# Two transformer-like blocks on one core: the order of the attention heads' vector work, the wait ahead of the first head, and one product for the position bias

## The chip, the cores and the metric

The kernel runs on one core of a Trainium2 chip. The metric is the device time of one execution in microseconds (us). The kernel before takes 866.2 us (median of 3 runs, 864.95 to 867.63).

## The reference, cut to what matters

The program computes a block of three parallel branches (local attention with a position bias, retention, attention to a memory), a gated feed-forward part with a short convolution, and after it two more layers. Sequence length is 256, model width 1024. The change lies in the first block's first stage. What is computed there, shortened:

```
n = rmsnorm(x, g_mix)
q_a, k_a, v_a, q_r, k_r, v_r, g_r, q_m, z_a, z_r, z_m = split(n @ w_in)
# local attention, 8 heads of 64; one block of 256 covers the whole sequence
s_own = q_a @ k_a.T * 64**-0.5 + table[:, rel_bucket(i - j)]   # table = rel_bias.T, 32 buckets x 8 heads
s_own = where(i >= j, s_own, -1e30);  y_a = softmax(s_own) @ v_a
# retention, 4 heads of 128: scores * decay, @ v, then a normalization of each row (mean, variance)
# memory attention, 4 heads of 128: softmax(q_m @ k_m.T * 128**-0.5) @ v_m
merged = sigmoid(z_a) * (y_a @ w_br_attn) + sigmoid(z_r) * (y_r @ w_br_ret) + sigmoid(z_m) * (y_m @ w_br_mem)
```

The position bias of a head is a function of i - j alone: a row of 384 numbers holds it for all distances that occur, and the 128 x 256 tile that a head adds is that row, read with a start that moves by one from partition to partition.

## The kernel before, in words

All large products run on TensorE in single-precision parts: each weight piece (128 x 2048 numbers, 1 MB) is loaded into `raw`, ScalarE (ACT) writes its rounded high part `whi` (L1117), and VectorE (DVE) subtracts to get the low part `wlo` (L1603). TensorE makes three passes over each piece (L452 to L454 where tokens lie on the output's partitions): 24 matmuls of 512 columns. There are 124 pieces, in a ring of three buffers. The cast of piece p+2 waits until piece p-1 has been multiplied; the subtraction waits for the cast; the load of the piece that reuses the buffer, issued from SyncE (SP), waits for the subtraction (L431).

Every engine runs one loop over the same steps, one step for each piece, in an order written out by hand. Step p is what stands ahead of and beside piece p. Pieces 0 to 3 are the memory's keys and values, 4 to 19 the first eight 512-wide chunks of `w_in` (two pieces each; chunk 0 is q_a, 1 is k_a, 2 is v_a), 20 to 31 its gates, 32 to 37 the branches' output products.

The heads run in a pipeline beside the pieces. There are 16 of them: local heads 0 to 7 start at steps 10 to 17, retention heads at 18 to 21, memory heads at 22 to 25. A head that starts at step n is turned (transposed) at step n, scored at n+1, its probabilities are turned at n+2 (not for retention), and it is weighed with the values at n+3. TensorE does, at the start of step p and ahead of piece p: `head_weigh` (L706), `head_prob_turn` (L684), `head_score` (L658 to L665), `head_turn` (L639), and each waits for what it needs from the step before. Vector work of step p is `head_dve(p)` (L1823): it normalizes the head that was weighed (for retention heads a chain of some twenty small operations, L1831 to L1844), adds the bias and takes the maximum of the head that was scored (L1866 to L1875; L1860 and L1872 for the other kinds), and copies the turned head out of PSUM (L1880). ACT's `head_act` takes the exponentials (L1271) and copies the turned probabilities (L1263). In DVE's loop the subtraction stands ahead of the head work:

```
                if p not in LATE_SPLIT:
                    split(p + 2)
                head_dve(p)
```

`head_turn` of the first head waits for ACT to have emptied chunk 2 of `w_in` (L625), the values, which piece 9 ends.

The position bias is made in steps 3 to 9, a head in each of steps 3 to 8 and two in step 9 (`rel_heads`). For each head GpSimd (POOL) copies its column of the table to 128 columns (`relw`, L2238), TensorE multiplies that with a constant 33 x 384 selection (`rel_rows`, L718), so that all 128 rows of the result are equal, ACT copies it to `brows` (L1254) and POOL stores it to memory as 128 rows (L2241). Two heads share the buffers by turns; TensorE's next product waits for ACT's copy of the last (L715), ACT's copy waits for the store before the last (L1253). After all eight, POOL loads each head's 128 x 256 tile `bias` from memory with rows that start one number apart (L2251). The first use of `bias` is DVE's at step 11 (L1865).

Of the kernel before, what the change touches and what calls it, by code (L numbers as in the profile page):

```python
# [15 lines left out]
P = 128  # L16
D = 1024
S = 256
T = S // P
# [59 lines left out]
def c0(name):  # L79
    return FIRST[name][1]  # L80
# [58 lines left out]
    return None  # L139


def rel_heads(n):


    return {9: (6, 7)}.get(n, (n - 3,) if 3 <= n < 9 else ())


LATE_SPLIT = (p0("up"), p0("xp") - 1, p0("xp"), p0("xp") + 1, p0("cu") - 1, p0("cu"), p0("cu") + 1)
# [13 lines left out]
def program(nc, ins, out):  # L162
    ctx = ExitStack()
    with ctx:
        def sb(name, shape, dt=F32):
            return ctx.enter_context(nc.sbuf_tensor(name, shape, dt))
# [4 lines left out]
        def overlay(size, *groups):  # L171

            made = []
            for group in groups:
# [44 lines left out]
        [[bias, decay, rcos, rsin, onehot, brows], [poolb, mtri, mmla, invf, sel, rows, csin, ccos, ang, kpr]] = overlay(  # L219
            8192 + RET_H * TRI * 4 + 1024 + 3 * TRI * 4,  # L220
            [("bias", [P, MOBA_H, S], F32), ("decay", [P, RET_H, TRI], F32), ("rcos", [P, T, 64], F32),
             ("rsin", [P, T, 64], F32), ("onehot", [P, TRI], F32), ("brows", [P, 2, TRI], F32)],
            [("poolb", [P, 4, T, S], F32), ("mtri", [P, S], F32), ("mmla", [P, TRI], F32),
             ("invf", [P, 32], F32), ("sel", [P, ML_H, P], F32),
             ("rows", [8, 5, S], F32),
# [3 lines left out]
        par = sb("par", [P, NPAR])  # L229
        half = sb("half", [P, 20])  # L230
        relb = sb("relb", [P, MOBA_H])
        relw = sb("relw", [P, 2, P])
        stats = sb("stats", [P, 32])
        rstd = sb("rstd", [P, 32])
        hrstd = sb("hrstd", [P, 3, T])
# [16 lines left out]
        qss = sb("qss", [P, T, MLA_H])  # L252
        kpss = sb("kpss", [P, T])
        rqk = sb("rqk", [P, 2, T, MLA_H])

        ones = relw[:, 0, :]

        hm = [qk_t[:, i, :].rearrange("p (t d) -> p t d", t=T) for i in range(2)]

# [26 lines left out]
        s_memt = [s_memt, sem("mem_columns_loaded_2")]  # L286
        s_ss, s_turn, s_thi, s_tlo = (sem(n) for n in (
            "squares_summed", "turned", "turned_hi", "turned_lo"))
        s_rb, s_rbw, s_rbs, s_bias = (sem(n) for n in (
            "rel_rows", "rel_lhs", "rel_rows_copied", "bias_loaded"))  # L290
        s_rbd = [sem(f"rel_rows_stored{i}") for i in range(2)]
        s_jt, s_jte, s_js, s_jse, s_jx, s_jp, s_jpe, s_jo, s_jn = (sem(n) for n in (
            "head_turned", "head_turned_copied", "head_scored", "scores_biased", "probs_ready",
            "probs_turned", "probs_turned_copied", "head_weighed", "head_done"))
# [27 lines left out]
        s_memset = sem("memset")  # L322
        s_store = sem("out_stored")

        scratch = nc.dram_tensor("bias_rows", (MOBA_H, P * TRI), F32, kind="Internal").ap()

        def pcol(name, i=0):
# [119 lines left out]
        def _(pe):  # L447
# [167 lines left out]
            def head_turn(p):  # L615

                if head_at(p) is None:
                    return
                kind, h = head_at(p)
                j = job(kind, h)  # L620
                if j not in TURNED:
                    return
                n = TURNED.index(j)
                if kind == "moba" and h == 0:
                    chunk_free(pe, c0("qkv") + 2)  # L625
                if kind == "ret" and h == 0:
                    pe.wait_ge(s_rot, 1)
                if kind == "mem" and h == 0:
                    chunk_free(pe, c0("qkv") + 7)
                if n >= 1:  # L630
                    pe.wait_ge(s_jte, n)
                else:
                    pe.wait_ge(s_rbs, MOBA_H)
                    pe.wait_ge(s_ident, 16)
                qs, ks = {"moba": (0, 1), "ret": (3, 4), "mem": (7, 8)}[kind]
                c = slice((h // 2 if kind == "moba" else h) * P, (h // 2 if kind == "moba" else h) * P + P)
                for i, s_ in enumerate((qs, ks)):
                    for t in range(T):
                        ins_ = nc.tensor.transpose(A[0][:, i * S + t * P:i * S + t * P + P],  # L639
                                                   tok[:, s_, t, c], ident[:, :])  # L640
                ins_.then_inc(s_jt, 1)
# [46 lines left out]
            def head_weigh(p):  # L688
                if head_at(p - 3) is None:
                    return  # L690
                kind, h = head_at(p - 3)
                j = job(kind, h)
                if j >= 1:
                    pe.wait_ge(s_jn, j)
                if kind == "ret":
                    pe.wait_ge(s_jse, j + 1)
                    chunk_free(pe, c0("qkv") + 5)
                    src = [(0, 0, 0), (1, 0, P), (1, 1, 2 * P)]
                    buf, vs, w = prob[:, j % 2, :], 5, P
                else:  # L700
                    pe.wait_ge(s_jpe, SMAX.index(j) + 1)
                    src = [(t, k, i * P) for i, (t, k, _) in enumerate(prob_blocks(kind))]
                    buf = prob_t[:, SMAX.index(j) % 2, :]
                    vs, w = (2, 64) if kind == "moba" else (9, P)
                for i, (t, k, col) in enumerate(src):
                    last = mm(A[3][:, t * P:t * P + w], buf[:, col:col + P],  # L706
                              tok[:, vs, k, h * w:h * w + w],
                              start=k == 0, stop=i + 1 == len(src) or src[i + 1][0] != t)
                last.then_inc(s_jo, 1)

            def rel_rows(h):

                pe.wait_ge(s_rbw, h + 1)
                if h >= 1:
                    pe.wait_ge(s_rbs, h)  # L715
                else:
                    pe.wait_ge(s_c1, 32)
                mm(A[3][:, 0:TRI], relw[0:33, h % 2, :], onehot[0:33, :],  # L718
                   start=True, stop=True).then_inc(s_rb, 1)


            def gate_logits():
                pe.wait_ge(s_gl, 1)
# [238 lines left out]

            first_piece()
            for p in range(1, Z0):
                for h in rel_heads(p):
                    rel_rows(h)
                head_weigh(p)
                head_prob_turn(p)
                head_score(p)
# [131 lines left out]
        def _(act):  # L1101
# [145 lines left out]
                                                        ACT.Copy, scale=gain(name, 2 * i + j))  # L1247
                    last.then_inc(s_thi, 1)

            def rel_copy(h):  # L1250
                act.wait_ge(s_rb, h + 1)
                if h >= 2:
                    act.wait_ge(s_rbd[h % 2], 16 * (h // 2))  # L1253
                nc.scalar.copy(brows[:, h % 2, :], A[3][:, 0:TRI]).then_inc(s_rbs, 1)  # L1254

            def head_act(p):

# [272 lines left out]
            for p in range(Z0):  # L1530
                if p not in LATE_SPLIT:
                    split(p + 2)
                empty(p - 1, True)
                for h in rel_heads(p):
                    rel_copy(h)
                head_act(p)
                ml_act(p)
                xc_act(p)
# [49 lines left out]
        def _(dve):  # L1588
# [588 lines left out]
            for p in range(Z0):  # L2177
                if p == p0("uq"):
                    mla_k()
                late(p)  # L2180
                if p == ML0 + 6:
                    ya_lo(p)
                if p not in LATE_SPLIT:
                    split(p + 2)
                head_dve(p)
                ml_dve(p)
                if p < ML0 + 6:
                    ya_lo(p)
                xc_dve(p)
                gates_dve(p)  # L2190
                if p == 2:
                    input_lo("mix", range(4))
                if p == 20:
                    dve.wait_ge(s_gh, 1)
                    V.tensor_tensor(wglo[:, :, :], wgate[:, :, :], wghi[:, :, :].bitcast(F32),
                                    ALU.subtract).then_inc(s_gl, 1)
                if p == p0("aout") - 1:
                    angles()
                boundary(p)
                for name, step in SCALED.items():  # L2200
                    if step == p:
                        normed(name)
                for name, which in turn_steps(p):
                    turn_lo(name, which)
                if p0("pool") - 3 <= p <= p0("pool"):
                    b = p - (p0("pool") - 3)
                    dve.wait_ge(s_mixhi, b + 1)
                    V.tensor_tensor(x1lo[:, 2 * b:2 * b + 2, :].rearrange("p k s -> p (k s)"),
                                    A[2 + b % 2][:, :],
                                    x1hi[:, 2 * b:2 * b + 2, :].rearrange("p k s -> p (k s)").bitcast(F32),  # L2210
                                    ALU.subtract).then_inc(s_mixlo, 1)
                if p == p0("ukv"):
                    mla_pe_k()
                if p == p0("uq") + 2:
                    mla_q_pe()
                empty(p)
# [4 lines left out]
        def _(pool):  # L2221
# [6 lines left out]
                i.then_inc(s_pool, 1)  # L2228
                pool.wait_ge(s_pool, count[0])

            Q.memset(relw[32:33, :, :], 1.0).then_inc(s_memset, 1)
            pool.wait_ge(s_memset, 1)

            pool.wait_ge(s_rel, 16)
            for h in range(MOBA_H):
                if h >= 2:
                    pool.wait_ge(s_rb, h - 1)
                Q.tensor_copy(relw[0:32, h % 2, :], relb[0:32, h:h + 1].broadcast_to([32, P])).then_inc(s_rbw, 1)  # L2238
                if h >= 1:
                    pool.wait_ge(s_rbs, h)  # L2240
                    pool.dma_start(scratch[h - 1].rearrange("(p n) -> p n", p=P), brows[:, (h - 1) % 2, :])\  # L2241
                        .then_inc(s_rbd[(h - 1) % 2], 16)
            pool.wait_ge(s_rbs, MOBA_H)
            Q.memset(ones, 1.0).then_inc(s_memset, 1)
            pool.dma_start(scratch[MOBA_H - 1].rearrange("(p n) -> p n", p=P), brows[:, (MOBA_H - 1) % 2, :])\
                .then_inc(s_rbd[(MOBA_H - 1) % 2], 16)
            for i in range(2):
                pool.wait_ge(s_rbd[i], 16 * MOBA_H // 2)

            for h in range(MOBA_H):  # L2250
                pool.dma_start(bias[:, h, :], scratch[h, P - 1:P - 1 + P * (TRI - 1)]  # L2251
# [210 lines left out]
```

## Time and profile before

| what | value |
|---|---|
| median of 3 runs | 866.2 us |
| the profiled execution's own time | 867.28 us |
| its span, first to last instruction | 865.5 us |
| mean granted TensorE clock | 0.982 of full |
| TensorE matmuls busy | 813.2 us (94%) |
| DVE, ACT, POOL busy | 566.2, 434.6, 141.5 us |

The span is some 1.8 us shorter than the execution's own time; this is what lies around the instructions. A TensorE busy for 94% of the span with a clock at 98% says that what can be won without less arithmetic lies in its gaps, in matmuls that could be left out, and in stretches at the lower clock. Times in the timeline count from the span's start.

### The profile page before, as it was taken

To read this page: it belongs to the slowest core of one execution; us is meant where nothing else is said; L and a number is where in the kernel's file an instruction comes from. 1 tells how busy PE (TensorE), PEld (TensorE's weight loads), DVE (VectorE), ACT (ScalarE), POOL (GpSimd) and SP (SyncE) were. 2 spreads that over 40 slices of the span, in tenths; PEclk is the share of its full clock that TensorE was granted. 3 is DMA by queue.
4 is the path that set the end of the run, shared out by engine and by line. 5 is a ranking of instruction groups with operands and counts; after the bars stand their busy time and mean duration, and the time that the engine had idled before them with its cause. 6 is when DMAs were issued, how large, how long until landed. Compare 5 with 4: busy or idle time off the path is not lost.

```text
span 865.5 us, 11958 instructions
## 1 busy us (share of the span) xinstructions
PE 813.2 (94%) x4614; PEld 700.7 (81%) x4614; DVE 566.2 (65%) x944; ACT 434.6 (50%) x589; POOL 141.5 (16%) x104
## 2 busy tenths in 40 slices
PE   3999999997999999999999999989999989997988
PEld 2676778875888889999988888989898868875767
DVE  3642455586456778778784476669764896876754
ACT  3752445323444457556653373646545345784441
POOL 1032480000000001544442000030410000062000
PEclk9998999999999999999999999999999999998999
DMA  9765444432445447555544535434655223652101
GB/s 354 290 227 190 147 145 146 146 105 91 147 145 195 165 176 283 176 179 195 190 168 181 194 146 192 148 144 146 211 192 182 98 102 134 250 195 97 49 1 49
DMA packets 22164, 142.24 MB, mean 164 GB/s; under 512 B 3040, under 2 KB 3936, under 8 KB 5728
## 3 DMA queue, kind: packets, MB, share of 16 engines
q1 hardware_dynamic: 19296, 134.51, 43.5%
q10 hardware_dynamic: 1920, 4.38, 1.3%
q0 software_dynamic: 896, 2.62, 0.9%
q8 instruction: 37, 0.61, 0.3%
q14 instruction: 15, 0.12, 0.0%
HBM read 138.88 MB, written 2.62 MB: 163 GB/s over the span
## 4 chain that ended last, share of the span: by engine, by line
PE 78%; DVE 8%; ACT 6%; issue 3%; DMA 2%; POOL 2%; SPq 0%; POOLq 0%; ACTq 0%; DVEq 0%
PE gemm L452 15%; PE gemm L454 15%; PE gemm L453 15%; PE gemm L458 8%; PE gemm L460 8%; PE gemm L459 8%; ACT whi L1117 3%; DVE wlo L1603 3%; DMA raw<-in_weights 2%; PE head L518 1%; PE head L718 1%; PE head L855 1%; PE head L756 1%; POOL pe_t L2303 1%; PE head L854 1%
## 5 line engine op out<-in xcount | busy, mean ns | idle before, releaser
L1603 DVE TENSOR_TENSOR wlo<-raw,whi 128x2048 fp32r<-128x2048 f32 x123 | 284.5, 2314 | 185.2 <-ACT whi L1117 184.8
L1117 ACT CAST whi<-raw 128x2048 fp32r<-128x2048 f32 x123 | 234.2, 1905 | 205.2 <-PE gemm L454 110.6
L452 PE MATMUL gemm<-whi,x0hi 128*128 128x512 f32 (+2 forms) x400 | 159.4, 398 | 0.0
L454 PE MATMUL gemm<-whi,x0lo 128*128 128x512 f32 (+2 forms) x400 | 155.1, 388 | 0.0
L453 PE MATMUL gemm<-wlo,x0hi 128*128 128x512 f32 (+2 forms) x400 | 155.0, 388 | 0.0
L458 PE MATMUL gemm<-x1hi,whi 128*128 128x256 f32 x400 | 113.9, 285 | 3.0 <-DVE om L2163 2.3
L460 PE MATMUL gemm<-x1hi,wlo 128*128 128x256 f32 x400 | 113.2, 283 | 0.0
L459 PE MATMUL gemm<-x1lo,whi 128*128 128x256 f32 x400 | 113.2, 283 | 0.0
L452 PEld LDWEIGHTS gemm<-whi,x0hi 128*128 128x128 f32 x400 | 76.3, 191 | 18.7 <-issue 5.1
L454 PEld LDWEIGHTS gemm<-whi,x0lo 128*128 128x128 f32 x400 | 75.9, 190 | 15.3
L453 PEld LDWEIGHTS gemm<-wlo,x0hi 128*128 128x128 f32 x400 | 76.2, 191 | 13.5
L458 PEld LDWEIGHTS gemm<-x1hi,whi 128*128 128x128 f32 x400 | 76.7, 192 | 3.6 <-DVE om L2163 2.5
L459 PEld LDWEIGHTS gemm<-x1lo,whi 128*128 128x128 f32 x400 | 76.8, 192 | 0.0
L460 PEld LDWEIGHTS gemm<-x1hi,wlo 128*128 128x128 f32 x400 | 76.7, 192 | 0.0
L2275 POOL TENSOR_TENSOR ubuf<-gbuf,ubuf 128x512 f32<-128x512 f32 x11 | 33.4, 3035 | 234.2 <-DVE ubuf L2120 234.2
L452 PE MATMUL gemm<-whi,x1hi 128*128 128x512 f32 x96 | 40.2, 419 | 16.0 <-DVE wlo L1797 13.4
L458 PE MATMUL gemm<-x0hi,whi 128*128 128x256 f32 x192 | 55.0, 286 | 0.0
L460 PE MATMUL gemm<-x0hi,wlo 128*128 128x256 f32 x192 | 54.3, 283 | 0.0
L459 PE MATMUL gemm<-x0lo,whi 128*128 128x256 f32 x192 | 54.3, 283 | 0.0
L453 PE MATMUL gemm<-wlo,x1hi 128*128 128x512 f32 x96 | 38.9, 405 | 0.0
L454 PE MATMUL gemm<-whi,x1lo 128*128 128x512 f32 x96 | 38.9, 405 | 0.0
L1271 ACT ACTIVATE prob<-prob,nmax 128x256 f32<-128x256 f32 (+1 forms) x24 | 11.2, 465 | 53.6 <-DVE nmax L1875 53.6
(339 smaller groups left out, 1398.2 us busy)
## 6 DMA issues: line engine op xcount, KB each, us to landing
raw<-in_weights SPq DMA_DIRECT2D x124, 1024.0 KB, 4.8
bias_rows<-brows POOLq DMA_DIRECT2D x8, 192.0 KB, 2.2
memt<-in_memt SPq DMA_DIRECT2D x2, 512.0 KB, 5.8
tok<-in_mem SPq DMA_DIRECT2D x1, 1024.0 KB, 11.3
xt<-in_xt SPq DMA_DIRECT2D x1, 1024.0 KB, 19.0
xres<-in_x ACTq DMA_DIRECT2D x1, 1024.0 KB, 9.2
bias<-bias_rows POOLq DMA_DIRECT2D x8, 128.0 KB, 2.3
poolb<-in_poolb ACTq DMA_DIRECT2D x1, 1024.0 KB, 5.5
```

Source lines behind the costliest of these rows:

```text
L452: mm(o, xh, wh, start=start, stop=False)
L453: mm(o, xh, wl, start=False, stop=False)
L454: return mm(o, xl, wh, start=False, stop=stop)
L458: mm(o, wh, xh, start=start, stop=False)
L459: mm(o, wh, xl, start=False, stop=False)
L460: return mm(o, wl, xh, start=False, stop=stop)
L518: ins_ = nc.tensor.transpose(b[:, j * S + t * P:j * S + t * P + P], turn_source(name, t, 2 * i + j), ident[:, :])
L718: mm(A[3][:, 0:TRI], relw[0:33, h % 2, :], onehot[0:33, :], start=True, stop=True).then_inc(s_rb, 1)
L1117: nc.scalar.copy(whi[:, p % RING, :], raw[:, p % RING, :]).then_inc(s_hi, 1)
L1271: i = nc.scalar.activation(prob[:, j % 2, a:b], prob[:, j % 2, a:b], ACT.Exp, bias=nmax[:, n % 4, t:t + 1], scale=1.0, accum_out=psumr[:, ...
L1603: V.tensor_tensor(wlo[:, p % RING, :], raw[:, p % RING, :], whi[:, p % RING, :].bitcast(F32), ALU.subtract).then_inc(s_lo, 1)
L2275: Q.tensor_tensor(u, gbuf[:, i % 2, :, :], u, ALU.mult).then_inc(s_h, 1)
```

## The change

Three edits. First, DVE does the heads' work of a step ahead of the subtraction of that step. Second, the first head's turn waits for the keys' chunk and not for the values' chunk; the wait for the values stands at the first weighing, three steps later. Third, the bias rows of all eight heads come from one product whose stationary side is the table itself (33 x 8), at step 3; ACT copies 8 rows; POOL stores these (12 KB), and after that has landed copies each row 128 times from memory to memory in one transfer (8 x 128 rows of 1536 bytes). POOL's column copies fall away, and the tile `ones` is written first. The eight loads of `bias` are the same, but wait for these two transfers.

```
-def rel_heads(n):
-    return {9: (6, 7)}.get(n, (n - 3,) if 3 <= n < 9 else ())
+REL_STEP = 3
...
                 if kind == "moba" and h == 0:
-                    chunk_free(pe, c0("qkv") + 2)
+                    chunk_free(pe, c0("qkv") + 1)
...
                 else:
-                    pe.wait_ge(s_rbs, MOBA_H)
+                    pe.wait_ge(s_rbs, 1)
                     pe.wait_ge(s_ident, 16)
...
                     vs, w = (2, 64) if kind == "moba" else (9, P)
+                    if j == 0:
+                        chunk_free(pe, c0("qkv") + 2)
...
-            def rel_rows(h):
-                pe.wait_ge(s_rbw, h + 1)
-                if h >= 1:
-                    pe.wait_ge(s_rbs, h)
-                else:
-                    pe.wait_ge(s_c1, 32)
-                mm(A[3][:, 0:TRI], relw[0:33, h % 2, :], onehot[0:33, :],
-                   start=True, stop=True).then_inc(s_rb, 1)
+            def rel_rows():
+                pe.wait_ge(s_memset, 1)
+                pe.wait_ge(s_rel, 16)
+                pe.wait_ge(s_c1, 32)
+                mm(A[3][0:MOBA_H, 0:TRI], relb[0:33, :], onehot[0:33, :], start=True, stop=True).then_inc(s_rb, 1)
...
-                for h in rel_heads(p):
-                    rel_rows(h)
+                if p == REL_STEP:
+                    rel_rows()
...
-            def rel_copy(h):
-                act.wait_ge(s_rb, h + 1)
-                if h >= 2:
-                    act.wait_ge(s_rbd[h % 2], 16 * (h // 2))
-                nc.scalar.copy(brows[:, h % 2, :], A[3][:, 0:TRI]).then_inc(s_rbs, 1)
+            def rel_copy():
+                act.wait_ge(s_rb, 1)
+                nc.scalar.copy(brows[0:MOBA_H, :], A[3][0:MOBA_H, 0:TRI]).then_inc(s_rbs, 1)
...
+                head_dve(p)
                 if p not in LATE_SPLIT:
                     split(p + 2)
-                head_dve(p)
...
+            order(Q.memset(ones[:, :], 1.0))
+            Q.memset(relb[32:33, :], 1.0).then_inc(s_memset, 1)
+            pool.wait_ge(s_rbs, 1)
+            pool.dma_start(rows_out, brows[0:MOBA_H, :]).then_inc(s_rbd, 16)
+            pool.wait_ge(s_rbd, 16)
+            pool.dma_start(scratch.rearrange("h (p n) -> h p n", p=P),
+                           rows_out.unsqueeze(1).broadcast_to([MOBA_H, P, TRI])).then_inc(s_rbd, 16)
+            pool.wait_ge(s_rbd, 32)
```

## Rows read from the trace of the kernel before

**Rows 1.** The page: TensorE's busy time, share of the span and instructions.
```profile
PE 813.2 (94%) x4614; PEld 700.7 (81%) x4614; DVE 566.2 (65%) x944; ACT 434.6 (50%) x589; POOL 141.5 (16%) x104
```
**Rows 2.** The page: the chain that ended last, share of the span by engine.
```profile
PE 78%; DVE 8%; ACT 6%; issue 3%; DMA 2%; POOL 2%; SPq 0%; POOLq 0%; ACTq 0%; DVEq 0%
```
**Rows 3.** TensorE's waits, 0 to 270 us: total us, times, longest us.
```profile
PE head L706 <- DVE tok L1844: 4.8, 3, 2.1
PE head L684 <- ACT prob L1271: 2.9, 2, 1.6
...
PE head L718 <- ACT brows L1254: 1.7, 1, 1.7
PE head L639 <- ACT tok L1445: 1.4, 1, 1.4
PE head L518 <- DVE x1lo L1820: 0.8, 2, 0.6
```
**Rows 4.** Timeline, first matmul of pieces 7 and 8: start us, us, what.
```profile
63.03 0.50 PE L452 MATMUL gemm<-whi,x0hi 128*128 128x512 f32 x1
...
69.55 0.50 PE L452 MATMUL gemm<-whi,x0hi 128*128 128x512 f32 x1
```
**Rows 5.** Timeline, start of piece 29, and what follows three pieces later.
```profile
243.83 0.48 PE L452 MATMUL gemm<-whi,x0hi 128*128 128x512 f32 x1
...
260.27 0.60 PE L518 MATMUL head<-ident,tok 128*128 128x128 f32 x4
```
**Rows 6.** Timeline, start of piece 9, first head's turn, start of piece 10.
```profile
79.35 0.79 PE L452 MATMUL gemm<-whi,x0hi 128*128 128x512 f32 x1
...
88.88 0.66 PE L639 MATMUL head<-ident,tok 128*128 128x128 f32 x4 [1.36 <-ACT tok L1445]
89.29 0.47 PE L452 MATMUL gemm<-whi,x0hi 128*128 128x512 f32 x1
```
**Rows 7.** Windows, 79 to 84 us: busy by engine, PEclk, DMA share, GB/s.
```profile
79.00:84.00 5.00, 5.00 (x12) 3.68 (x12) 0.61 (x1) 0.48 (x1) 0.69 (x2) 0.50 0.72 226
```
**Rows 8.** The page, DMA issues: KB each, median us from issue to landing.
```profile
raw<-in_weights SPq DMA_DIRECT2D x124, 1024.0 KB, 4.8
bias_rows<-brows POOLq DMA_DIRECT2D x8, 192.0 KB, 2.2
```
**Rows 9.** The tile view of `bias_rows`: its transfers' time to landing.
```profile
DMA to landing us min/median/max: 2.1/2.3/5.2
```
**Rows 10.** Timeline, TensorE's head work at steps 21, 23 and 25, and the pieces.
```profile
169.94 0.83 PE L706 MATMUL head<-tok,prob 128*128 128x128 f32 x6
...
171.62 0.47 PE L452 MATMUL gemm<-whi,x0hi 128*128 128x512 f32 x1
...
188.12 0.83 PE L706 MATMUL head<-tok,prob 128*128 128x128 f32 x6
...
190.01 0.48 PE L452 MATMUL gemm<-whi,x0hi 128*128 128x512 f32 x1
...
220.11 1.05 PE L706 MATMUL head<-tok,prob_t 128*128 128x128 f32 x8
...
222.66 0.48 PE L452 MATMUL gemm<-whi,x0hi 128*128 128x512 f32 x1
```
**Rows 11.** Timeline, DVE at steps 22 and 23, and TensorE's turn behind it.
```profile
180.45 2.29 DVE L1603 TENSOR_TENSOR wlo<-raw,whi 128x2048 fp32r<-128x2048 f32 x1 [0.68 <-ACT whi L1117]
...
182.66 0.49 DVE L1831 BATCH_NORM_STATS2 bn<-head 128x6 f32<-128x128 f32 x2
...
187.41 0.68 DVE L1880 COPY qk_t<-head 128x512 f32<-128x512 f32 x1
...
192.52 0.49 DVE L1831 BATCH_NORM_STATS2 bn<-head 128x6 f32<-128x128 f32 x2
...
198.18 0.68 DVE L1880 COPY qk_t<-head 128x512 f32<-128x512 f32 x1
...
199.45 0.66 PE L684 MATMUL head<-ident,prob 128*128 128x128 f32 x4 [1.57 <-ACT prob L1271]
```

More of the change, by code:

```diff
@@ L221, in program @@
             [("bias", [P, MOBA_H, S], F32), ("decay", [P, RET_H, TRI], F32), ("rcos", [P, T, 64], F32),
-             ("rsin", [P, T, 64], F32), ("onehot", [P, TRI], F32), ("brows", [P, 2, TRI], F32)],
+             ("rsin", [P, T, 64], F32), ("onehot", [P, TRI], F32), ("brows", [P, TRI], F32)],
             [("poolb", [P, 4, T, S], F32), ("mtri", [P, S], F32), ("mmla", [P, TRI], F32),
@@ L231, in program @@
         relb = sb("relb", [P, MOBA_H])
-        relw = sb("relw", [P, 2, P])
+        ones = sb("ones", [P, P])
         stats = sb("stats", [P, 32])
@@ L254, in program @@
         rqk = sb("rqk", [P, 2, T, MLA_H])
-        ones = relw[:, 0, :]
         hm = [qk_t[:, i, :].rearrange("p (t d) -> p t d", t=T) for i in range(2)]
@@ L288, in program @@
             "squares_summed", "turned", "turned_hi", "turned_lo"))
-        s_rb, s_rbw, s_rbs, s_bias = (sem(n) for n in (
-            "rel_rows", "rel_lhs", "rel_rows_copied", "bias_loaded"))
-        s_rbd = [sem(f"rel_rows_stored{i}") for i in range(2)]
+        s_rb, s_rbs, s_rbd, s_bias = (sem(n) for n in (
+            "rel_rows", "rel_rows_copied", "rel_rows_stored", "bias_loaded"))
         s_jt, s_jte, s_js, s_jse, s_jx, s_jp, s_jpe, s_jo, s_jn = (sem(n) for n in (
@@ L323, in program @@
         s_store = sem("out_stored")
+        rows_out = nc.dram_tensor("bias_row", (MOBA_H, TRI), F32, kind="Internal").ap()
         scratch = nc.dram_tensor("bias_rows", (MOBA_H, P * TRI), F32, kind="Internal").ap()
@@ L1533, in _ @@
                 empty(p - 1, True)
-                for h in rel_heads(p):
-                    rel_copy(h)
+                if p == REL_STEP:
+                    rel_copy()
                 head_act(p)
@@ L2229, in order @@
                 pool.wait_ge(s_pool, count[0])
[L2231 to L2248, printed above, removed]
+            order(Q.memset(ones[:, :], 1.0))
[6 more added lines that the diff above has]
+            pool.wait_ge(s_rbd, 32)
             for h in range(MOBA_H):
```

## The prediction

> **What bounds the kernel now.** I read the page first: TensorE's matmuls are busy 94% of the span [rows 1], and the chain that ended last is TensorE for 78%, DVE for 8%, ACT for 6% [rows 2]. So an edit counts by what it takes from TensorE's queue or from its gaps. Next came the table of TensorE's waits up to 270 us, where all touched lines lie. Four of its rows belong to the heads and the bias: weighing waits for DVE's retention result (4.8 us in 3), the turn of probabilities for ACT's exponentials (2.9 in 2), a bias product for ACT's copy (1.7), and the first head's turn for the values (1.4) [rows 3]. These waits are only part of the price, since the clock falls behind some of them: from 79 to 84 us the granted clock is 0.50, the 1.2 GHz level, right after the 1.7 us in which TensorE stood for the bias product [rows 3, 7]. So I went to the timeline and took differences between starts, which hold wait and clock together.
>
> **Undisturbed prices.** Pieces 29 to 31 run with nothing between them: 16.44 us from the first matmul to what follows, so 5.48 us each [rows 5]. Ahead of a piece, the head work of retention step 21 takes 171.62 - 169.94 = 1.68 us, that of step 23 (retention weighed, memory scored) 1.89, that of step 25 (all memory, four parts) 2.55 [rows 10].
>
> **Bias products, steps 4 to 8.** With one product between them, pieces 7 and 8 start 69.55 - 63.03 = 6.52 us apart [rows 4]. Without it, 5.48. That is 1.04 us for each of five steps: 5.2 us. The product at step 3 stays; it has 8 rows instead of 128, but streams the same 384 columns, so I give it no gain (bounds: 0 and the whole 1.04). What could be next: the weights. ACT's cast of piece p+2 starts at the end of piece p-1, and cast and subtraction (about 4.2 us) fit into the two pieces, 10.96 us, that remain. A load is issued behind the subtraction, 4.2 us into a step, lands 4.8 us later [rows 8], and its cast isn't due before 3 x 5.48 = 16.4 us: 7 us of slack. So the shorter steps are kept.
>
> **Steps 9 and 10.** Pieces 8 and 9 start 79.35 - 69.55 = 9.80 us apart [rows 4, 6]; two products stand there, the second waits for ACT's copy of the first, and ACT is at a cast. Without them 5.48: 4.3 us. Piece 9 then runs at the lower clock and the turn waits for the values: 89.29 - 79.35 = 9.94 us to piece 10 [rows 6]. Piece 9 at full clock is 5.5, the turn with its wait gone is 89.29 - 88.88 = 0.41: 5.9 in all, 4.0 us less. The new wait for the keys' chunk is met: that chunk ends with piece 7 and ACT empties it during piece 8. The wait for the values, now ahead of weighing at step 13, is met three steps earlier. It would have TensorE's whole queue behind it, but for nothing.
>
> **DVE's order, retention and memory steps.** All of the waits for DVE's retention result, and the two for exponentials, lie at steps 22 to 25 [rows 3, 10, 11]; at the local heads the order is worth almost nothing. Before, from step 21's weighing (169.94) to step 25's (I count to the start of step 26, 220.11 [rows 10]) 50.2 us pass. Now the same stretch worked out in the new order, with t = 0 at step 21's start. Durations: DVE's head work at steps 21 and 22 is 182.66 to 188.09, 5.43 us; at step 23 and 24 the scores are ready for ACT 5.66 us after its start (192.52 to 198.18) and it ends after 6.34; a subtraction is 2.29; the probabilities can be turned 199.45 - 198.18 = 1.27 us after the scores are ready [rows 11].
> Step 21: weighed at 0.75, DVE's head work ends 6.2, subtraction 8.5.
> Step 22 starts on TensorE at 1.68 + 5.5 = 7.2; DVE's head work, 8.5 to 13.9, subtraction to 16.2.
> Step 23 starts at 14.4 (it needs DVE's 13.9: no wait). DVE: scores ready 21.9, end 22.5, subtraction to 24.8; probabilities at 23.1.
> Step 24 starts at 14.4 + 1.89 + 5.5 = 21.8; weighing is done at 22.4 (0.7 us), then 0.7 us of waiting for 23.1, then 1.66 for turn, score and turn, piece to 30.3. DVE: 24.8, scores ready 30.5, probabilities 31.8, subtraction to 33.5.
> Step 25: weighing to 31.2 (0.9), wait 0.6, 1.66, piece: step 26 starts at 38.9.
> So 50.2 - 38.9 = 11.3 us. In this stretch DVE needs 7.7 us and more for each step against TensorE's 7.2, so it falls behind step by step; that is where the two waits that I expect come from. The subtraction that is moved back has the load of the buffer behind it on SP's queue: it ends 1.3 to 3.2 us into the next step, and its piece is needed two steps later, so nothing waits. At steps 10 to 20 it ends about 6 us into its own step instead of 4.2, within the slack above. Bounds for the stretch: if both small waits vanish 12.6; if each of four steps keeps a wait of 1.5 us and one piece falls to the low clock as piece 9 did (9.94 - 0.41 - 1.36 - 5.5 = 2.7 us [rows 6]), 11.3 + 1.3 - 6 - 2.7 = 3.9. I take 11.3, since it follows from the rows.
>
> **Turns behind the heads.** TensorE also waits twice, 0.8 us in all, to turn the branches' results at steps 27 and 29, for low parts that DVE makes behind the subtraction and the head work [rows 3]. With the head work earlier ACT's high part is earlier too: I take the 0.8 (0 to 0.8).
>
> **The new transfers.** ACT's copy of step 3 keeps its place: three steps of 6.52 us ahead of piece 7 [rows 4] piece 4 starts, at 63.0 - 19.6 = 43.5 us. The 12 KB store takes about 2.2 us, as the 192 KB one does [rows 8]; no row shows a memory-to-memory copy. From below, 8 x 192 KB = 1.5 MB at the weights' rate (1 MB in 4.8 us) [rows 8] is 7.2 us; from above, eight times the slowest store of a head, 5.2 us [rows 9], 42 us. I take 15, the nearer to the weights' row, doubled for reading and writing memory. Then the eight loads, unchanged; one behind the other at 2.2 us, as the stores, they are 18 us at most, and overlapped about 7, which I take: all in at 43.5 + 2.2 + 15 + 7 = 68 us. Piece 10 starts 13.5 us earlier than its 89.29, at 75.8, step 11 at 81.3; TensorE minds from about 84.5, when maxima and exponentials (2.5 us) would be late for step 12 at 87. So it is hidden, with 16 us to spare, and so are the loads of weights that share the engines with it. Without that cover each us late is a us.
> The Trainium skill, DMA: Bandwidth & Descriptors, Rules for kernel authors, says that a transfer whose slowest dimension has fewer than 16 entries is confined to at most so many of the 16 engines; the copy's is 8. No row before shows such a transfer. By that rule the copy takes twice my lower bound, 14.4 us, and weights loaded beside it are slowed on half of the engines; the sum stays, the chance of a late bias grows.
>
> **Sum.** 5.2 + 4.3 + 4.0 + 11.3 + 0.8 = 25.6 us. Against the profiled execution's own 867.28 us, which is 1.1 above the median, that gives 841.7; against the median of 866.2, 840.6 us. All behind step 29 is the same work in the same order and shifts as a whole.
>
> **Rivals.**
> - DVE stays the bound at steps 22 to 25 (3.9 instead of 11.3 us). For it: DVE has more work there than a step of TensorE is long, and the order doesn't lessen it. Against it: only four steps, and DVE enters them without arrears. Time: 840.6 + 7.4 = 848.0.
> - The bias isn't there in time. For it: a copy of a kind that no row shows, beside the weights' loads. Against it: 16 us of room. With 42 us for the copy, all is in at 95: 10.5 us late, and 2.7 for the clock: 853.8.
> - Steps 4 to 9 are bound by the loads of weights once the products are gone. Against it: 7 us of slack in each load, and pieces 29 to 31 run at 5.48 with loads of the same size [rows 5]. Half of the 9.5 us would be lost: 845.
> - Slower than before: the copy of the bias takes so long that the wait at step 11, with piece 13's subtraction and all that follows behind it on DVE, eats the gain. It decides once all is in at 84.5 + 25.6 = 110 us or later, a copy of 57 us or more; with 65 us the wait is 33 us and the time 876 with the clock.
>
> **How the numbers follow.** The forecast has 0.75, with its own range 837 to 844. DVE as bound has 0.12, late bias 0.06, loads 0.04, slower than before 0.02, and 0.01 is for no effect. The range reaches from 836 to 850: it takes in the first and the third rival. A difference under 0.3%, 2.6 us, can't be told from no change here. Faster 0.96, within 0.3% 0.02, slower 0.02.
>
> **What would show it.** One L718 group at step 3, and first matmuls of pieces 4 to 9 about 5.5 us apart; no clock of 0.5 near 80 us; piece 10 starting near 76 us. The big copy landing before 65 us. Between the weighings of steps 21 and 26 about 39 us, with only two waits for L1271 there, under 1 us each, and none for L1844. I am wrong if TensorE waits for L1844 or L1880 at steps 22 to 24, if DVE waits for `bias` at step 11, or if ACT's casts wait for `raw`.

## The result and the profile after

The changed kernel takes 842.25 us (median of 4 runs, 841.38 to 844.52) against 866.91 us (4 runs): ratio 0.9727, 95% interval 0.9698 to 0.9757. In a second comparison it took 841.95 us (6 runs). The forecast was 840.6 us, 836 to 850. The profiled execution has a span of 842.6 us, 22.9 less than before. Line numbers have moved: L703 is now the weighing (before L706), L679 the turn of probabilities (L684), L713 the bias product (L718), L634 the heads' turn (L639), L513 the branches' turn (L518), L447 to L449 the passes (L452 to L454), L1595 the subtraction (L1603).

First the page, engines and the chain that ended last; they answer to [rows 1, 2].

```profile
PE 800.3 (95%) x4600; PEld 697.0 (83%) x4600; DVE 567.0 (67%) x944; ACT 432.1 (51%) x582; POOL 127.8 (15%) x90
...
PE 81%; DVE 7%; ACT 4%; DMA 3%; issue 2%; POOL 2%; SPq 0%; POOLq 0%; ACTq 0%; DVEq 0%
```

Fourteen matmuls are gone (seven products of two) and the share of TensorE on the chain has grown. Now TensorE's waits in the first 260 us, which answer to [rows 3].

```profile
PE gemm L447 <- DVE wlo L1789: 13.8, 1, 13.8
PE gemm L447 <- DVE wlo L1595: 3.8, 2, 2.2
PE head L513 <- DVE x0lo L1812: 0.3, 1, 0.3
```

The first two lie at pieces 0 to 3, where the inputs come in. All five rows of [rows 3] are gone; what is left of such waits ahead of the heads' matmuls is 0.15 us and less, too short for the table of waits. The timeline shows the starts of pieces 7, 8 and 10, the first head's turn, and the weighings of steps 21 and 26; it answers to [rows 4, 6, 10].

```profile
60.77 0.39 PE L447 MATMUL gemm<-whi,x0hi 128*128 128x512 f32 x1
...
66.22 0.39 PE L447 MATMUL gemm<-whi,x0hi 128*128 128x512 f32 x1
...
77.10 0.60 PE L634 MATMUL head<-ident,tok 128*128 128x128 f32 x4
77.45 0.47 PE L447 MATMUL gemm<-whi,x0hi 128*128 128x512 f32 x1
...
157.51 0.83 PE L703 MATMUL head<-tok,prob 128*128 128x128 f32 x6
...
196.10 1.05 PE L703 MATMUL head<-tok,prob_t 128*128 128x128 f32 x8
```

Pieces 7 and 8 start 5.45 us apart instead of 6.52. The turn has nothing in brackets: no wait. The weighings of steps 21 and 26 are 196.10 - 157.51 = 38.6 us apart instead of 50.2. DVE in steps 22 and 23, with the subtraction now behind the head work, answers to [rows 11]:

```profile
165.93 0.49 DVE L1823 BATCH_NORM_STATS2 bn<-head 128x6 f32<-128x128 f32 x2
...
170.67 0.68 DVE L1872 COPY qk_t<-head 128x512 f32<-128x512 f32 x1
171.27 2.28 DVE L1595 TENSOR_TENSOR wlo<-raw,whi 128x2048 fp32r<-128x2048 f32 x1
173.47 0.49 DVE L1823 BATCH_NORM_STATS2 bn<-head 128x6 f32<-128x128 f32 x2
```

From one normalization to the next 173.47 - 165.93 = 7.54 us pass, and from 164 to 182 us DVE has no wait long enough for the table of waits: it is occupied through these steps. At last the transfers, from the page; they answer to [rows 8, 9].

```profile
raw<-in_weights SPq DMA_DIRECT2D x124, 1024.0 KB, 4.8
bias_rows<-bias_row POOLq DMA_DIRECT2D x1, 1536.0 KB, 17.6
...
bias<-bias_rows POOLq DMA_DIRECT2D x8, 128.0 KB, 4.0
```

Over the whole trace, the lead of a kernel over the kernel before is how much earlier the same piece starts, so a minus is a loss. It can be taken apart by stretches. Each column is one profiled execution, set against the one profiled execution of the kernel before (867.28 us). For the changed kernel and the first four experiments, in us:

| stretch (starts of pieces) | changed | e1 order | e2 wait | e3 bias | e4 order from 21 |
|---|---|---|---|---|---|
| lead at piece 3 | -1.92 | -0.72 | -0.37 | -1.84 | -2.23 |
| 3 to 9 | 9.61 | 0.09 | -0.01 | 9.61 | 0.12 |
| 9 to 10 | 4.15 | -0.13 | 1.57 | 2.57 | -0.15 |
| 10 to 21 | 0.59 | 0.58 | -0.28 | -0.06 | -0.09 |
| 21 to 26 | 11.58 | 11.55 | 2.99 | 0.10 | 11.55 |
| 26 to 32 | 1.20 | 1.20 | 0.00 | 0.00 | 1.20 |
| 32 to the span's end | -2.4 | -2.3 | -0.7 | -1.8 | -2.3 |

### The profile page after: what moved, and what is told of

The parts are those of the page before. It is cut to its first block, busy times and chain, and to the rows that moved or that the text cites. A ratio compares the mean times of both kernels' runs of the same rounds, so it can differ in the third digit from the quotient of the medians.

```text
span 842.6 us, 11895 instructions
## 1 busy us (share of the span) xinstructions
PE 800.3 (95%) x4600; PEld 697.0 (83%) x4600; DVE 567.0 (67%) x944; ACT 432.1 (51%) x582; POOL 127.8 (15%) x90
## 4 chain that ended last, share of the span: by engine, by line
PE 81%; DVE 7%; ACT 4%; DMA 3%; issue 2%; POOL 2%; SPq 0%; POOLq 0%; ACTq 0%; DVEq 0%
PE gemm L447 16%; PE gemm L449 16%; PE gemm L448 16%; PE gemm L453 8%; PE gemm L455 8%; PE gemm L454 8%; DMA raw<-in_weights 3%; DVE wlo L1595 2%; ACT whi L1110 2%; PE head L513 1%; PE head L703 1%; PE head L848 1%; PE head L749 1%; POOL pe_t L2285 1%; PE head L847 1%
## 5 line engine op out<-in xcount | busy, mean ns | idle before, releaser
L1595 DVE TENSOR_TENSOR wlo<-raw,whi 128x2048 fp32r<-128x2048 f32 x123 | 284.8, 2317 | 123.4 <-ACT whi L1110 123.0
L447 PE MATMUL gemm<-whi,x0hi 128*128 128x512 f32 (+2 forms) x400 | 157.4, 394 | 0.0
L449 PE MATMUL gemm<-whi,x0lo 128*128 128x512 f32 (+2 forms) x400 | 154.2, 385 | 0.0
L454 PE MATMUL gemm<-x1lo,whi 128*128 128x256 f32 x400 | 113.9, 285 | 0.0
L449 PEld LDWEIGHTS gemm<-whi,x0lo 128*128 128x128 f32 x400 | 75.4, 188 | 14.9
L447 PEld LDWEIGHTS gemm<-whi,x0hi 128*128 128x128 f32 x400 | 75.5, 189 | 14.7 <-issue 1.3
L454 PEld LDWEIGHTS gemm<-x1lo,whi 128*128 128x128 f32 x400 | 77.5, 194 | 0.0
L447 PE MATMUL gemm<-whi,x1hi 128*128 128x512 f32 x96 | 40.3, 420 | 17.6 <-DVE wlo L1789 13.8
L454 PE MATMUL gemm<-x0lo,whi 128*128 128x256 f32 x192 | 54.4, 283 | 0.0
L449 PE MATMUL gemm<-whi,x1lo 128*128 128x512 f32 x96 | 39.6, 412 | 0.0
L447 PEld LDWEIGHTS gemm<-whi,x1hi 128*128 128x128 f32 x96 | 19.4, 202 | 23.3 <-DVE wlo L1789 13.8
## 6 DMA issues: line engine op xcount, KB each, us to landing
bias_rows<-bias_row POOLq DMA_DIRECT2D x1, 1536.0 KB, 17.6
```

What stands on the lines that cost most here:

```text
L447: mm(o, xh, wh, start=start, stop=False)
L449: return mm(o, xl, wh, start=False, stop=stop)
L454: mm(o, wh, xl, start=False, stop=False)
L1595: V.tensor_tensor(wlo[:, p % RING, :], raw[:, p % RING, :], whi[:, p % RING, :].bitcast(F32), ALU.subtract).then_inc(s_lo, 1)
```

## The experiments

**e1, e2, e3: one part of the change each, and e4, the order at the retention heads only.** All four are the kernel before with one edit.

e1: DVE's order at all steps.
```
+                head_dve(p)
                 if p not in LATE_SPLIT:
                     split(p + 2)
-                head_dve(p)
```


> The kernel before with one edit: DVE does the heads' work ahead of the subtraction. Theory A (the three parts of the change act in different stretches and add up): all of the 11.6 us between the weighings of steps 21 and 26, some 0.6 us at steps 10 to 20 and 1.2 us at steps 27 to 31 are this edit's; 13.4 us less than before, 853.5 us; between those weighings 38 to 39 us instead of 50.2, and no wait for the retention result (L1844). The 0.50 clock near 80 us and the products at steps 3 to 9 stay. Theory B (the order pays only with the earlier bias): less than 8 us, and TensorE or DVE wait for the bias or for ACT's copies at steps 11 to 13.

e2: the place of the wait for the values.
```
-                    chunk_free(pe, c0("qkv") + 2)     # first head's turn
+                    chunk_free(pe, c0("qkv") + 1)
...
+                    if j == 0:                        # first head's weighing
+                        chunk_free(pe, c0("qkv") + 2)
```


> The kernel before with one edit: the first head's turn waits for the keys' chunk, its weighing for the values. Theory A: the 1.36 us wait ahead of the turn goes, nothing else; 1.4 us less, 865.5 us; piece 9 still runs at the lower clock, because TensorE's 1.7 us gap between the two products of step 9 is still there. Theory B (the low clock hangs on the wait for the values too): 4.1 us less, 862.8.

e3: the bias product and its transfers, as in the change (the changed kernel with the edits of e1 and e2 undone).

> The kernel before with the one product for the position bias and its new transfers, order of DVE and first head's wait as before. Theory A: 5.2 us at steps 4 to 8, 4.3 at step 9 and 2.7 of piece 9's lower clock: 12.2 us less, 854.7 us; the wait of 1.4 us for the values stays ahead of the first head's turn, with the clock at 1.00 behind it. Theory B (that wait of 1.4 us brings the clock down by itself once the gap ahead of it is gone): 9.5 us less, 857.4, and a stretch with a granted clock near 0.5 behind 76 us.

e4: head work first from step 21 on.
```
+                if p >= 21:
+                    head_dve(p)
                 if p not in LATE_SPLIT:
                     split(p + 2)
-                head_dve(p)
+                if not (p >= 21):
+                    head_dve(p)
```


> The kernel before with DVE's head work ahead of the subtraction at steps 21 to 28 only. Theory A (only the retention heads' normalization is long enough for the order to matter): 12.8 us less, 854.1 us, within 1 us of the kernel with the new order at all steps. Theory B (DVE must enter step 21 ahead, from the local heads' steps): between the weighings of steps 21 and 26 over 42 us remain, and over 3 us more than with the order at all steps.

Measured, against 864.38 us for the kernel before (13 runs): e1 856.65 us (4 runs), ratio 0.9874, 0.9806 to 0.9942; e2 864.11 (10 runs), 0.9989, 0.9958 to 1.0021; e3 856.73 (4 runs), 0.9872, 0.9806 to 0.9939; e4 858.98 (4 runs), 0.9894, 0.9826 to 0.9962. The medians of e1, e3 and e4 are 2 to 5 us above what theory A gave, and against the median beside them e1, e2 and e3 gain 7.7, 0.3 and 7.7 us: 15.7 together, where the whole change gained 24.7. With intervals of some 6 us on each side for e1 and e3 that doesn't contradict a sum of parts, but it doesn't show one. The stretches do: between pieces 3 and 32 e1 has 13.29 us, e3 12.22, and e2 1.57 at its own place, 27.1 together, and the changed kernel has 27.1. In one execution of each kernel the parts add up, each in its stretch. By these stretches theory A holds for e1, e3 and e4, theory B for none of them. e4 has the same 11.55 us at steps 21 to 26 as e1; the order at the local heads' steps brings 0.6 us. (The medians of e4 and e1 differ by 2.3 us, more than theory A's 1; of the 2.2 us between their spans 1.5 lie ahead of piece 3, where no head is at work yet.)

The waits of e3 between 0 and 260 us show what the bias product doesn't touch:

```profile
PE head L701 <- DVE tok L1834: 4.0, 3, 2.1
...
PE head L679 <- ACT prob L1261: 2.9, 2, 1.6
PE head L634 <- ACT tok L1435: 1.4, 1, 1.4
```

and those of e1 what the order does not:

```profile
PE head L718 <- ACT brows L1254: 1.7, 1, 1.7
PE head L639 <- ACT tok L1445: 1.4, 1, 1.4
PE head L684 <- ACT prob L1271: 0.3, 2, 0.2
```

In e2 theory A holds at the place of the edit: 1.57 us, and piece 9 stays at the low clock, so that does not hang on the wait for the values. e3, which takes the products away with their gap, has the full clock at piece 9. (It takes away all the products of steps 4 to 9; that it is the gap of step 9 and not the earlier products was not parted.) The windows of e2 (columns as in [rows 7]) behind that gap:

```profile
79.40:84.40 5.00, 5.00 (x12) 3.70 (x12) 0.59 (x1) 0.48 (x1) 0.69 (x2) 0.50 0.73 231
```

At step 11 e2 gives 0.24 us back: TensorE now waits there for the first head's turned copy (0.2 us for L1882), which in e2 is still behind the subtraction. In e3 the wait of 1.36 us is there and the clock behind it is 1.00, against theory B:

```profile
75.00:80.00 5.00, 3.64 (x19) 2.78 (x18) 1.07 (x1) 2.78 (x3) 0.00 (x0) 1.00 0.80 275
80.00:85.00 5.00, 5.00 (x24) 3.94 (x23) 2.89 (x2) 0.52 (x2) 0.00 (x0) 1.00 0.24 80
```

The 2.99 us of e2 at steps 21 to 26 are hardly the edit's: its instructions there are those of the kernel before. The same window of both, first the kernel before:

```profile
176.00:184.00 8.00, 6.44 (x26) 5.11 (x25) 6.86 (x21) 3.05 (x3) 0.00 (x0) 0.79 0.36 133
```

```profile
176.00:184.00 8.00, 6.44 (x34) 5.09 (x32) 6.84 (x21) 3.05 (x3) 0.00 (x0) 1.00 0.33 116
```

Both have 1.56 us of idle TensorE in the window; in one the clock fell, in the other not. From 208 to 216 us the kernel before is at 0.79 again, and e2 is at 1.00 there after 0.85 from 192 to 200 us; over the whole stretch TensorE waits 4.8 us for the retention results in the one and 2.3 in the other.

This bears on what the order is worth. Its 11.6 us are measured against an execution that needed 3.0 us more in this stretch than e2's did; against one like e2's the order brings 8.6 us. So of the 27.1 us 3.0 belong to how the kernel before happened to run. How often it runs one way or the other isn't known.

**e5: the copy of the bias rows on all DMA engines.**
```
-            pool.dma_start(scratch.rearrange("h (p n) -> h p n", p=P),
-                           rows_out.unsqueeze(1).broadcast_to([MOBA_H, P, TRI]))
+            pool.dma_start(scratch.rearrange("h (p n) -> p h n", p=P),
+                           rows_out.unsqueeze(0).broadcast_to([P, MOBA_H, TRI]))
```


> The changed kernel, with the memory-to-memory copy of the bias rows written so that the 128 copies of a row are the slowest dimension instead of the 8 heads. In the changed kernel it took 17.6 us from issue to landing. Theory A (a slowest dimension of 8 keeps the copy on 8 of the 16 DMA engines, as the Trainium skill says): it lands in 8 to 11 us; the loads of weights beside it are no slower than the 4.8 us median; the time doesn't change, since the bias has some 13 us to spare. Theory B (the copy is slow because both its ends are in memory): 15 us or more again.

It lands in 11.9 us instead of 17.6, as the page's row of e5 says, and the time is 843.57 us (1 run), as near to the changed kernel's as its executions are to each other; e5's lead over the changed kernel stays between 0.88 and 0.97 us from piece 5 to piece 112.

```profile
bias_rows<-bias_row POOLq DMA_DIRECT2D x1, 1536.0 KB, 11.9
```

So most of theory A: with the dimension of 8 outermost the copy is slower, though not by a factor of two, and it missed theory A's 8 to 11 us by 0.9. The records of the single packets in the traces say why. Their times add up to nearly the same, 66.9 us in the changed kernel and 65.1 in e5, but from the first packet's start to the last one's end 13.3 us pass against 7.4, a factor of 1.8; the commonest number of packets under way at once is 8 in the one (for 3.0 of the 13.3 us) and 16 in the other (1.8 of 7.4). Some 4 us from the issue to the first packet are the same in both (3.9 and 4.2) and bring the factor down to 1.5. The Trainium skill (DMA: Bandwidth & Descriptors, Rules for kernel authors) states that an outermost dimension smaller than 16 confines a transfer to at most so many engines. The traces agree, with 8 and 16 packets at a time and 17.6 against 11.9 us; they don't name the engine of a packet.

Undisturbed loads beside the copy, which theory A also expected, weren't seen: of the loads of weights issued from 38 to 72 us the median is 7.3 us here and 7.4 in the changed kernel, against 5.0 in the kernel before in the same stretch and 4.8 over the whole trace. They have the slack for it.

**e6, e7: the copy two and three times,** one after the other, in the changed kernel.
```
+            for i in range(2):          # e6; in e7 range(3)
+                pool.dma_start(...).then_inc(s_rbd, 16)
+                pool.wait_ge(s_rbd, 32 + 16 * i)
```


> The changed kernel, but the memory-to-memory copy is made twice, the second once the first has landed. Theory (the bias is hidden as long as all of it is in by about 87 us, when step 12 asks for probabilities): all in at 71 + 18 = 89 us; DVE waits some 4 us for it at step 11, TensorE 1 to 3 us at step 12, and 2.7 us more if the clock falls; 1 to 6 us slower in the stretch from piece 11 to piece 13 than the changed kernel's 14.7 us. Rival (more room than worked out): nothing.

> The changed kernel, with the copy made three times in a row. Theory: all in at 71 + 35 = 106 us, TensorE waits about 19 us at step 12 with DVE's wait for the bias as releaser behind ACT's exponentials, and 2.7 us for the clock: the stretch from piece 11 to piece 13 takes 34 to 37 us instead of 14.7; the whole gain of the change is nearly eaten. Rival (DVE can catch up, since the subtraction behind the wait has slack): under 15 us lost.

e6 takes 850.23 us, e7 859.41 (1 run each). DVE's and TensorE's waits from 60 us on, first of e6, then of e7:

```profile
DVE prob L1858 <- DMA bias<-bias_rows: 8.1, 1, 8.1
...
PE head L679 <- ACT prob L1263: 3.6, 2, 3.5
```

```profile
DVE prob L1858 <- DMA bias<-bias_rows: 19.2, 1, 19.2
...
PE head L679 <- ACT prob L1263: 14.7, 2, 14.5
```

Of DVE's wait all but some 4.6 us (8.1 - 3.5, 19.2 - 14.5) reach TensorE: that is the room between the scores of step 11 and step 12's need of probabilities. In pieces' starts e6 loses 6.5 us between pieces 11 and 13 and e7 16.9, the waits of 3.5 and 14.5 and on top of them a stretch at the low clock (0.53 from 92 to 99 us in e6). e6's theory gave 1 to 6 and is missed by half a us: DVE goes on at 90.0 us, not at 89. e7's gave 19 to 22 and is missed by 2.4: its third copy took not 18 us but 10.9, at a time when nearly no weights were loaded; the next loads stood behind DVE's wait. DVE's waits end at 90.0 and 100.4 us, and less what TensorE waited that is 86.6 and 85.9: late bias is thus a real price of the change, from 86 to 87 us on. The changed kernel's eighth load is issued at 66.9 us and lands some 4 us later, 16 us before.

**e8: more work for DVE at the retention heads,** in the changed kernel.
```
+                        for _ in range(2):
+                            order(rsqrt(rsum[:, :], mv[:, :, 1], 1.0, T))
-                        order(rsqrt(rsum[:, :], mv[:, :, 1], 1.0, T))
```


> The changed kernel, with the retention heads' reciprocal square root computed twice (11 small DVE operations more for each of four heads, some 2.15 us each, 8.6 in all; the result is the same). Between the weighings of steps 21 and 26 the changed kernel needs 38.6 us. Theory A (DVE has nearly no room left there: 7.7 us of work for each step of 7.2): the stretch grows by 9 to 12 us, more than what is added, with waits for L1836 (the retention result) and for probabilities. Theory B (the order gave DVE slack, since the subtraction can be late by two steps): it grows by less than 4 us.

851.25 us (1 run). Steps 21 to 26 take 8.7 us longer for about 8.6 us of added work (7.4 us of it DVE's busy time on the page, the rest the pauses between the small operations). The clock is 1.00 all through. The waits from 60 to 260 us:

```profile
PE head L703 <- DVE tok L1837: 4.1, 3, 1.8
PE head L679 <- ACT prob L1263: 2.9, 2, 1.6
```

That is just under the 9 of theory A's range, where more than the added work was expected, and far over theory B's 4: DVE has no room there, and what is added comes out at the end one for one. The waits are nearly those of the kernel before [rows 3], now made by work and not by order.

**e9: the same edit at one more step, and e10, the changed kernel again beside it.** TensorE stands 2.30 us for DVE at the pooling product (piece 83), where a subtraction is ahead of the work that TensorE waits for.
```
-                if p not in LATE_SPLIT:
+                if p not in LATE_SPLIT and p != p0("pool"):
                     split(p + 2)
...
                 empty(p)
+                if p == p0("pool"):
+                    split(p + 2)
```


> The changed kernel, with the same edit at one more place: at the step of the pooling branch's product (piece 83), DVE subtracts for piece 85 behind that step's low parts and emptied chunks, not ahead of them. In the changed kernel TensorE stands 2.30 us there for DVE's om, and in some executions runs at the lower clock behind it, 1.5 us more. Theory A (the subtraction ahead is what makes DVE late, as at the retention heads): the wait goes or falls under 0.3 us, 2 to 3.8 us less than the changed kernel (median over executions about 3), so some 839 us. Rival (the chunk's low parts from ACT, or the next piece's low part, then come late): the wait moves to piece 84 or 85 and nothing is won.

> The changed kernel unaltered, beside the last one on the same chip. 842 us; the executions differ by up to 3 us, because the clock falls at some of the gaps in some executions and not in others.

Median e9 839.41 us (6 runs, 837.13 to 841.09), e10 841.95 us (6 runs, 840.91 to 843.91), before 867.49 (11 runs): ratios 0.9695 (0.9661 to 0.9729) and 0.9726 (0.9692 to 0.976). These intervals, both against the same runs of the kernel before, overlap; but five of e9's six runs are below the lowest of e10's, and the traces agree: at piece 83 e9 gains 3.5 us on the profiled execution of the changed kernel and 2.0 on e10's. TensorE's waits for DVE's `om`, first in the changed kernel, then in e9:

```profile
PE gemm L453 <- DVE om L2155: 2.3, 1, 2.3
```

```profile
PE gemm L453 <- DVE om L2155: 0.3, 1, 0.3
```

The wait is at theory A's 0.3 us and hasn't moved on: from piece 84 to piece 85 e9 takes 5.86 us, as e10 does. e9 is the fastest version, by 2.5 us of median.

## Why the prediction was right, step by step

**Bias products and step 9** (5.2 + 4.3 us): 9.61 us between pieces 3 and 9, in the changed kernel and in e3. Each of steps 4 to 8 gave 1.08 us but the first, which gave 0.93. The product at step 3 nearly kept its price: 0.84 us from its start to piece 3's before, 0.74 after.

**Step 10** (4.0 us): 4.15 us, and e2 and e3 part it into 1.57 for the wait and 2.57 for the low clock of piece 9. Both parts of the step as the prediction put it hold.

**DVE's order** (11.3 us): 11.58. The steps' times came out nearly as worked out: from weighing to weighing steps 21 to 26 take 38.6 us (forecast 38.9). That is the half of the difference which the mechanism fixes; the other half, 50.2 us, is a row of one execution, and in e2's the stretch took 3.0 us less. The prediction took that row without asking whether it repeats, so that 11.3 came so near is in part luck. DVE's head work at step 22 began 165.93 - 164.74 = 1.2 us behind that step's weighing (forecast 1.3), at step 23 1.5 us (1.8). The two waits that I expected for exponentials are there, but 0.3 us each ahead of the weight load (0.15 and 0.13 ahead of the matmul) instead of 0.7 and 0.6, since head work and subtraction follow each other in 7.54 us and not in the 7.72 that I had. The rival that DVE stays the bound was nearer than its 0.12 says: e8 shows that it is the bound, with TensorE just behind; by e8's one for one, I estimate that 0.5 us more in each step would have been paid in full too. (The third row of [rows 10] is step 26's, not step 25's: a branch's turn stands there in place of a head's, of the same 0.60 us, so the sum doesn't move.)

**What I had at almost nothing:** the order at steps 10 to 20 brought 0.59 us, and the turns behind the heads 1.20 instead of 0.8.

**The bias's way:** copy 17.6 us (I took 15), all in near 71 us (68). Hidden, as forecast; e6 and e7 put the edge at 86 to 87 us (84.5 in the prediction). The 15 had no row of its kind behind it: doubling the weights' rate for reading and writing memory stands on nothing measured, and what the packets show is the dimension of 8. The loads of weights beside the copy went from 5.0 to 7.4 us and stayed hidden, as forecast, within the 7 us of slack that it had worked out. The rivals of a late bias and of one that makes the kernel slower had their mechanism right; e7, late by all of two copies, still ends 8.6 us faster than the kernel before ran beside it.

**The sum.** 25.6 us was forecast for stretches that gave 27.1. The span of the profiled execution fell by 22.9, the median by 24.7. The difference lies outside the change: 1.9 us at the start, 1.5 of it at piece 2, which ran at the low clock (as in e3, e4, e6, e8 and e10, not in e1, e2, e5, e7 and e9), and 2.4 later, 1.5 of it at piece 83 alone. That the time came out within 2 us of the forecast owes something to luck too: the touched stretches gave 1.5 us more than forecast, and the 4.3 lost elsewhere were in no sum. At piece 83 the kernel before and the changed one have the same wait of 2.30 us for DVE, and then this, first before, then changed:

```profile
572.00:576.00 4.00, 4.00 (x35) 3.85 (x34) 1.75 (x4) 1.91 (x3) 0.00 (x0) 1.00 0.41 170
```

```profile
546.80:550.80 4.00, 4.00 (x23) 3.76 (x22) 1.36 (x4) 0.43 (x1) 0.00 (x0) 0.57 0.42 178
```

35 matmuls in 4 us against 23. All twelve profiled executions but e9's have this wait; piece 83 then takes 8.9 us in the kernel before, e1, e2, e8 and e10, and 10.4 in the changed kernel and e3 to e7. e10 is the changed kernel itself, and e4 has nothing of the new bias, so it goes with none of the edits. What decides it in an execution stays open; no experiment was made on that.

## What to carry to other kernels

- In a pipeline in which one engine does both short work that the next step waits for and long work that is due only two steps later, put the short work first; before doing so, sum that engine's work for a step, because what is won ends where this sum passes the step of the bounding engine. The same pattern stood at a second place (e9) and gave 2 us more.
- Take price and gain as differences between starts of the same piece, not as waits: the wait table had 4.8 + 2.9 us for the retention stretch, and 11.6 came out. Part of the rest is the low clock behind the waits; but in e8, at full clock, waits of 4.1 + 2.9 us go with 8.7 us lost, so the table falls short of the price even there.
- A gain read from one execution's rows holds for that execution: take the kernel before from more than one, where its clock falls in the stretch. Where gaps bring the clock down in some executions only, single parts of a change are better told apart in the trace, stretch by stretch, than by whole times.

## What the runs showed of the hardware that I had not expected

- The same gap on TensorE doesn't always bring the clock down: after 2.30 us of waiting the granted clock was 1.00 in one execution and 0.57 in another, and of eleven executions with this wait six took 1.5 us more for the piece behind it. After the 1.36 us in e3 the clock stayed at 1.00; behind the gap at 77 us it was 0.50 in the kernel before and in e2. In steps 21 to 26 the profiled execution of the kernel before, with two drops of the clock, took 3.0 us more than that of e2, with the same instructions and one drop.
- One copy of 1.5 MB within memory took 17.6 us with the 8 heads as outer dimension and 11.9 with 128 rows there, beside loads of weights; most often 8 and 16 packets were under way at once. In e7, with nearly no loads beside it, the copy over 8 took 10.9, with 8 packets under way for 5.7 of its packets' 7.9 us.
- While such a copy runs, 1 MB loads of weights take about 7.4 us instead of 5.0 (the same stretch of the kernel before), whichever of the two forms the copy has.
